# Neighbour attention's keys in groups of half a tile, and four smaller changes of order in a two-block transformer kernel

## Time and profile before

| | |
|---|---|
| three runs | 1334.83, 1334.91, 1335.91 us |
| the profiled execution's own time | 1333.72 us |
| its span in the trace | 1332.2 us |
| granted clock of PE, mean | 0.993 |
| PE busy | 1291.9 us, 97% of the span |
| DVE busy | 741.3 us, 56% |
| ACT busy | 474.2 us, 36% |
| POOL busy | 607.7 us, 46% |
| DMA | 105.40 MB, 79 GB/s in the mean |
| chain that ended last | PE 88%, DVE 4%, issue 3%, POOL 3%, ACT 1%, DMA 1% |

### The profile page before, as it was taken

One profiled execution on the slowest core, in us unless ns is written; L12 is line 12 of the kernel. 1 busy time (PEld: TensorE's weight loads), 2 busy tenths in 40 slices (PEclk: granted clock), 3 DMA queues, 4 the chain that ended last, 5 costly groups with the idle time before them and its releaser, 6 DMA issues.

```text
span 1332.2 us, 20250 instructions
## 1 busy us (share of the span) xinstructions
PE 1291.9 (97%) x6918; PEld 1050.4 (79%) x6918; DVE 741.3 (56%) x1372; ACT 474.2 (36%) x1010; POOL 607.7 (46%) x367
## 2 busy tenths in 40 slices
PE   7999999999899999999999999999999999999997
PEld 6877777877688888888888788888877888888765
DVE  4236867566855454533436677876526555555541
ACT  3233333422422222221114566666104444554520
POOL 5523323238354444445551444444367656666421
PEclk9999999999999999999999999999999999999999
DMA  6422222233233333332233211111143222222202
GB/s 179 113 59 83 65 79 64 64 89 107 65 108 89 99 90 99 90 102 88 87 103 96 63 50 32 47 47 48 35 134 106 62 76 76 75 64 74 63 26 69
DMA packets 196561, 105.40 MB, mean 79 GB/s; under 512 B 18982, under 2 KB 194444, under 8 KB 196508
## 3 DMA queue, kind: packets, MB, share of 16 engines
q1 hardware_dynamic: 196060, 104.00, 27.4%
q0 software_dynamic: 432, 0.69, 0.3%
q10 hardware_dynamic: 16, 0.00, 0.0%
HBM read 102.57 MB, written 2.10 MB: 79 GB/s over the span
## 4 chain that ended last, share of the span: by engine, by line
PE 88%; DVE 4%; issue 3%; POOL 3%; ACT 1%; DMA 1%; SPq 0%; DVEq 0%; POOLq 0%; ACTq 0%
PE ps L365 20%; PE ps L366 20%; PE ps L367 20%; PE ps L396 8%; POOL w_low L344 1%; PE ps L1389 1%; PE ps L1359 1%; PE ps L1370 1%; PE ps L1122 1%; PE ps L1392 1%; PE ps L1140 1%; PE ps L936 1%; PE ps L378 1%; PE ps L1141 1%; PE ps L1142 1%
## 5 line engine op out<-in xcount | busy, mean ns | idle before, releaser
L344 POOL TENSOR_TENSOR w_low<-w_raw,w_high 128x1024 fp32r<-128x1024 f32 x180 | 437.5, 2432 | 472.9 <-DVE w_high L339 461.0
L365 PE MATMUL ps<-h_high,w_high 128*128 128x512 f32 x816 | 333.1, 408 | 5.2 <-POOL w_low L344 3.7
L366 PE MATMUL ps<-h_low,w_high 128*128 128x512 f32 x816 | 323.6, 397 | 0.0
L367 PE MATMUL ps<-h_high,w_low 128*128 128x512 f32 x816 | 322.2, 395 | 0.0
L339 DVE CAST w_high<-w_raw 128x1024 fp32r<-128x1024 f32 x183 | 160.3, 878 | 98.1 <-DMA w_raw<-in_w_in_dram 36.7
L365 PEld LDWEIGHTS ps<-h_high,w_high 128*128 128x128 f32 x816 | 154.0, 189 | 46.5 <-issue 5.4
L367 PEld LDWEIGHTS ps<-h_high,w_low 128*128 128x128 f32 x816 | 154.2, 189 | 35.2
L366 PEld LDWEIGHTS ps<-h_low,w_high 128*128 128x128 f32 x816 | 154.1, 189 | 34.1 <-issue 2.6
L1654 ACT ACTIVATE z<-ps,cv 128x512 f32<-128x512 f32 x42 | 32.7, 778 | 156.3 <-PE ps L367 156.3
L2248 DVE SCALAR_TENSOR_TENSOR z<-ps,cv,z 128x511 f32<-128x511 f32 x42 | 31.5, 749 | 96.8 <-ACT z L1654 96.8
L366 PE MATMUL ps<-m_low,w_high 128*128 128x512 f32 x176 | 69.4, 395 | 0.0
(11 more groups left out here) (363 smaller groups left out, 2438.2 us busy)
## 6 DMA issues: line engine op xcount, KB each, us to landing
w_raw<-in_w_in_dram SPq DMA_DIRECT2D x150, 256.0 KB, 3.2
w_raw<-in_w_up_dram SPq DMA_DIRECT2D x88, 256.0 KB, 3.2
w_raw<-in_w_out_dram SPq DMA_DIRECT2D x44, 256.0 KB, 3.0
w_raw<-in_w_down_dram SPq DMA_DIRECT2D x32, 256.0 KB, 3.0
w_raw<-in_w_down_dram SPq DMA_DIRECT2D x16, 192.0 KB, 2.6
rel<-in_rel_bias_dram SPq DMA_DIRECT2D x8, 384.0 KB, 3.2
x_tok<-in_x_dram SPq DMA_DIRECT2D x4, 512.0 KB, 5.9
w_raw<-in_w_ob_dram SPq DMA_DIRECT2D x8, 256.0 KB, 2.9
```

The costliest lines, as they stand in the source:

```text
L344: pool.tensor_tensor(w_low[:, n % RING, :], w_raw[:, n % RAW, :], w_high[:, n % RING, :].bitcast(F32), ALU.subtract).then_inc(low_made, 1)
L365: pe.matmul(acc, wh, mh, start=first and k == 0, stop=False)
L366: pe.matmul(acc, wh, ml, start=False, stop=False)
L367: done = pe.matmul(acc, wl, mh, start=False, stop=last and k == tiles - 1)
```

## The change

- **Neighbour attention.** In a tile the tokens lie as (column, row), so that 8 columns are 64 tokens that follow one another. Each tile sees keys by half tiles: the widths with meta keys are 224, 272, 272 and 208. Keys are laid out once with the meta keys repeated between them (`nk_n`, 5 pieces); whole groups of 128 are 1, 2, 2, 1; what is left at either end, up to 80 rows with the meta keys, is turned as one group and weighed against `nv_end`. v is turned in three whole groups and two ends. The bias table has 6 additions for each head (4 of 128 elements, 2 of 64) that read and write with steps of 16 and 8 elements. In `weigh`, each half has two products over whole groups, of 256 and 128 columns, in place of three. `copy_b` waits for `turn`, no more for `copy_a`. Where the tokens are placed, loaded or stored (`x_t`, mask, `rel`, cos and sin, `out`) the order is changed to match; `rel` comes in a DMA for each head, and a store's outermost index is the column, 16 long.
- **Feed-forward.** DVE casts strip `N_UP+3` before `norm_dve`; in the first `up_turn` the casts are those of `N_UP+4`, `+5` and `+6`.
- **Last latent head.** `y_rounded` runs on each half; the low part is subtracted on DVE by halves (`m_y_rest`), no more on POOL.
- **POOL's order.** The wait for `tables_in` comes after the lows of `N_OM+6` and `N_OM+7`. In the first pair alone the table of the next pair stands behind `squares_low(i, c + 1, 0)`, not before it.

The diff, without buffer declarations, semaphore counts and blank lines:

```
-NA_W = [2 * P, 3 * P, 3 * P, 2 * P]
-NA_G = [0, 0, 1, 2]
-NA_OFF = [2 * META + 3 * P, 0, META, 3 * META + 5 * P]
-NA_COLS = 4 * META + 7 * P
-NA_WIN = [META, META, 0, 0]
-NA_META = [0, 0, 3 * P, 2 * P]
+HALF_TILE = P // 2
+END = META + HALF_TILE
+NA_W = [END + META + P, META + 2 * P, META + 2 * P, P + END]
+NA_K = [0, END, END + META + P, END + META + 2 * P]
+NA_KEYS = 2 * END + META + 3 * P
+NA_OFF = [0, END + META + P, END + 2 * META + P, END + 3 * META + 3 * P]
+NA_COLS = 2 * END + 3 * META + 4 * P
+NA_FULL = [1, 2, 2, 1]
+NA_WIN = [END + META, META, 0, 0]
+NA_META = [0, 0, 2 * P, P]
...
-return ps[:, 2:4, :].rearrange("p b (a h q) -> p (b a) h q", h=2, q=P)[:, 0:n]
+return ps[:, 2, 0:n * 2 * P].rearrange("p (a h q) -> p a h q", h=2, q=P)
...
+def half_tiles(ap, first, n):
+    dims = [[1, 8], [16, 8]]
+    if n > 1:
+        dims = [[P - 8, 2]] + dims
+    return bass.AP(tensor=ap.tensor, offset=ap.offset + first, ap=[list(d) for d in ap.ap[:-1]] + dims)
...
+def by_columns(ap):
+    return ap.rearrange("p (g r c) -> p g c r", r=8, c=16)
+def tiles(ap):
+    return ap.rearrange("p (g c r) -> p g c r", c=16, r=8)
...
-sp.dma_start(mask[:], c_mask).then_inc(s["tables_in"], 16)
+sp.dma_start(mask[:], c_mask.rearrange("(r c) k -> c r k", c=16)).then_inc(s["tables_in"], 16)
...
-sp.dma_start(rel[:], rel_bias[0:2].rearrange("h q k -> q h k")).then_inc(s["rel_in"], 16)
+for h in range(2):
+    sp.dma_start(rel[:, h, :], rel_bias[h].rearrange("(r c) k -> c r k", c=16)).then_inc(s["rel_in"], 16)
...
-dst = out[0].rearrange("(r g c) d -> g r c d", g=CG, c=16)[t]
+dst = out[0].rearrange("(r g c) d -> g c r d", g=CG, c=16)[t]
 sp.dma_start(dst[:, :, d], y_tok[:, t, d]).then_inc(s["out_stored"], 16)
...
-y_parts(3, 1)
...
 z_ = c % 2
...
-    for o, m, r in ((META, 0, 0), (NA_OFF[0] + META, 3 * P, P), (NA_OFF[3], 5 * P, 0)):
-        w = 3 * P if m == 0 else 2 * P
-        pool.tensor_tensor(nb[:, z_, h, o:o + w], rel[:, h, r:r + w],
-                           mask[:, m:m + w], ALU.add).then_inc(s["nb_ready"], 1)
-for o in (0, META + 3 * P, NA_OFF[0], NA_OFF[3] + 2 * P):
+    for o, m, r, n in ((NA_OFF[1] + META, 8, 8, 2), (NA_OFF[1] + META + P, P + 8, P + 8, 2),
+                       (END + META, 3 * P + 8, P + 8, 2),
+                       (NA_OFF[3], 5 * P + 8, 8, 2), (META, 3 * P, P, 1),
+                       (NA_OFF[3] + P + META, 5 * P + P + 8, P + 8, 1)):
+        to = nb[:, z_, h, o:o + n * HALF_TILE]
+        if n > 1:
+            to = to.rearrange("p (b c r) -> p b c r", c=8, r=8)
+        else:
+            to = to.rearrange("p (c r) -> p c r", r=8)
+        pool.tensor_tensor(to, half_tiles(rel[:, h, :], r, n), half_tiles(mask[:], m, n), ALU.add)\
+            .then_inc(s["nb_ready"], 1)
+for o in (0, NA_OFF[1], NA_OFF[2] + 2 * P, NA_OFF[3] + P):
     pool.tensor_copy(nb[:, z_, :, o:o + META],
...
 if more:
     ahead = N_NA + 4 * (c + 2)
-    bias_table(i, c + 1)
+    if c:
+        bias_table(i, c + 1)
     squares_low(i, c + 1, 0)
+    if c == 0:
+        bias_table(i, c + 1)
     make_low(pool, ahead, i * 8)
...
-pool.wait_ge(s["tables_in"], 64)
 for n in range(N_OM + 6, N_OM + 8):
     make_low(pool, n)
+pool.wait_ge(s["tables_in"], 64)
+pool.memset(np_end[:], 0.0)
+pool.memset(nb[:, :, :, END:END + META], -1e30)
 bias_table(0, 0)
...
-w, k0 = META + NA_W[t], (0, 0, META + P, META + 2 * P)[t]
...
 def turn(i, c, t):
     pe.wait_ge(s["t_probs"], i * 8 + (4 * c + t + 1))
     if c or t:
+        pe.wait_ge(s["t_copied_a"], i * 8 + (4 * c + t))
+    for a in range(NA_FULL[t]):
+        for h in range(2):
+            o = (2 * a + h) * P
+            k = NA_WIN[t] + a * P
+            pe.transpose(ps[:, 2, o:o + P], ne[:, t % 2, h, k:k + P], ident[:])
+    if c or t:
         pe.wait_ge(s["t_copied_b"], i * 8 + (4 * c + t))
-    for a in range(NA_W[t] // P):
-        for h in range(2):
-            o = (2 * a + h) % 4 * P
-            k = NA_WIN[t] + a * P
-            pe.transpose(ps[:, 2 + a // 2, o:o + P], ne[:, t % 2, h, k:k + P], ident[:])
     for h in range(2):
-        mm = pe.transpose(ps[0:META, 3, (2 + h) * P:(3 + h) * P],
-                          ne[:, t % 2, h, NA_META[t]:NA_META[t] + META], ident[:])
+        mm = pe.transpose(ps[0:NA_ENDS[t], 3, h * P:(1 + h) * P],
+                          ne[:, t % 2, h, NA_META[t]:NA_META[t] + NA_ENDS[t]], ident[:])
     mm.then_inc(s["t_turned"], 1)
...
-for a, q in ((0, slice(0, 2 * P)), (1, slice(0, 2 * P)), (2, slice(P, 2 * P))) if p == 0 else \
-        ((1, slice(0, 2 * P)), (2, slice(0, 2 * P)), (0, slice(0, P))):
+for a, q in (((0, slice(0, 2 * P)), (1, slice(P, 2 * P))), ((1, slice(0, 2 * P)), (0, slice(0, P))))[p]:
...
 def turn_v(i, c):
     pe.wait_ge(s["nv_kept"], i * 2 + (c + 1))
-    for a in range(4):
-        pe.transpose(ps[:, 5, a * P:(a + 1) * P], nvf[:, META + a * P:META + (a + 1) * P], ident[:])
-    pe.transpose(ps[0:META, 6, 0:P], nvf[:, 0:META], ident[:]).then_inc(s["nv_turned"], 1)
+    for a in range(3):
+        pe.transpose(ps[:, 5, a * P:(a + 1) * P], nvf[:, END + a * P:END + (a + 1) * P], ident[:])
+    for e, of in enumerate((nvf[:, 0:END], nvf_end[:])):
+        mm = pe.transpose(ps[0:END, 6, e * P:(e + 1) * P], of, ident[:])
...
-act.activation(x_t[:, k, :].rearrange("p (g r c) -> p r g c", g=CG, c=16),
+act.activation(x_t[:, k, :].rearrange("p (g c r) -> p r g c", g=CG, c=16),
...
+def y_rounded(i, c, q=slice(0, S)):
+    act.wait_ge(s["s_y"], i * 4 + (2 * c + q.stop // (2 * P)))
...
+y_rounded(i, c, slice(0, 2 * P))
 m_copy(i, c, 3)
...
-y_rounded(3, 1)
+y_rounded(3, 1, slice(2 * P, S))
...
-act.activation(halves(nvf), wide(5), ACT.Copy).then_inc(s["nv_kept"], 1)
+act.activation(halves(nvf), wide(5), ACT.Copy)
+act.activation(nvf_end[:, 0:META], ps[:, 5, 0:META], ACT.Copy)
+act.activation(nvf_end[:, META:END], ps[:, 6, HALF - HALF_TILE:HALF], ACT.Copy).then_inc(s["nv_kept"], 1)
...
+make_high(dve, N_UP + 3)
 norm_dve(dve, 2, xs, V_FFN, S, hh, hl)
...
-make_high(dve, N_UP + 4 * c + m + 3, i * 4)
+if c:
+    make_high(dve, N_UP + 4 * c + m + 3, i * 4)
+elif m < 3:
+    make_high(dve, N_UP + m + 4)
...
 dve.wait_ge(s["qr_turned"], i + (c // 2 + 1))
-dve.tensor_tensor(turned, ps[:, 7, :], sin[:, META:L], ALU.mult).then_inc(s["qr_part"], 1)
...
+def m_y_rest(q, n):
+    dve.wait_ge(s["s_high"], n)
+    dve.tensor_tensor(y_low[:, 7, q], gy[:, q], y_high[:, 7, q].bitcast(F32), ALU.subtract)\
...
+m_y_rest(slice(0, 2 * P), 8)
 m_gated(i, c, 1)
+m_y_rest(slice(2 * P, S), 9)
...
-dve.tensor_tensor(kpe_root, k_pe, cos[:], ALU.mult).then_inc(s["pe_part"], 1)
+dve.tensor_tensor(kpe_root[:, 0:META], k_pe[:, 0:META], cos[:, 0:META], ALU.mult)
+dve.tensor_tensor(tiles(kpe_root[:, META:L]), tiles(k_pe[:, META:L]), by_columns(cos[:, META:L]), ALU.mult).then_inc(s["pe_part"], 1)
...
-dve.tensor_tensor(halves(kpe_sq), wide(0), halves(sin[:]), ALU.mult).then_inc(s["pe_part"], 1)
+dve.tensor_tensor(kpe_sq[:, 0:META], ps[:, 0, 0:META], sin[:, 0:META], ALU.mult)
+for b, at, o in ((0, META, META), (1, META + 2 * P, 0)):
+    p = dve.tensor_tensor(tiles(kpe_sq[:, at:at + 2 * P]), tiles(ps[:, b, o:o + 2 * P]),
+                          by_columns(sin[:, at:at + 2 * P]), ALU.mult)
+p.then_inc(s["pe_part"], 1)
...
-dve.tensor_copy(np_meta[:, :, q], ps[0:META, 3, 2 * P:4 * P].rearrange("p (h q) -> p h q", h=2))\
+dve.wait_ge(s["t_turned"], i * 8 + (4 * c + t + 1))
+n = NA_ENDS[t]
...
 def normed(i, c, m):
     dve.wait_ge(s["q_root"], i * 8 + (4 * c + 2 * m + 2))
-    dst = (nk_f[:, 0:L], nq_f)[m]
-    dve.scalar_tensor_tensor(dst, dst, (col(V_NK), nq_gain[:, 0:1])[m], root[:, m, 0:(L, S)[m]],
-                             ALU.mult, ALU.mult).then_inc(s["q_normed"], 1)
-    if m == 0:
-        dve.wait_ge(s["q_normed"], i * 6 + (3 * c + 1))
-        dve.tensor_copy(nk_f[:, L:L + META], nk_f[:, 0:META]).then_inc(s["q_normed"], 1)
+    if m == 1:
+        dve.scalar_tensor_tensor(nq_f, nq_f, nq_gain[:, 0:1], root[:, 1, 0:S], ALU.mult, ALU.mult)\
+            .then_inc(s["q_normed"], 1)
+        return
+    for to, at, n in ((0, 0, END), (END + META, END, 3 * P), (NA_KEYS - HALF_TILE, L - HALF_TILE, HALF_TILE),
+                      (END, 0, META), (NA_KEYS - END, 0, META)):
+        nk = dve.scalar_tensor_tensor(nk_n[:, to:to + n], nk_f[:, at:at + n], col(V_NK),
+                                      root[:, 0, at:at + n], ALU.mult, ALU.mult)
+    nk.then_inc(s["q_normed"], 2)
```

More of the change, by code:

```diff
@@ L1089, in kpe_turn @@
                 pe.wait_ge(s["pe_part"], 2)
-                for h in range(2):
-                    mm = pe.matmul(ps[:, h, 0:HALF], rot[:], k_pe[:, h * HALF:(h + 1) * HALF], start=True, stop=True)
-                mm.then_inc(s["pe_turned"], 1)
+                cut = META + 2 * P
+                pe.matmul(ps[:, 0, 0:cut], rot[:], k_pe[:, 0:cut], start=True, stop=True)
+                pe.matmul(ps[:, 1, 0:L - cut], rot[:], k_pe[:, cut:L], start=True, stop=True).then_inc(s["pe_turned"], 1)
```

(2 more changed lines are left out.)

66 lines of the change are left out of this document (36 added, 30 removed).

## The result

The changed kernel took 1304.67 us in the median of four runs (1303.55 to 1305.26), the kernel before 1334.95 in the median of four, one more than above (1334.83 to 1335.91). The ratio is 0.9771 with a 95% interval of 0.9754 to 0.9788. Predicted were 1304.0, from 1299 to 1314. The span of the profiled execution went from 1332.2 to 1301.8 us, 30.4 less; the working had 30.7. That is closer than the terms behind it deserve: three of them were off by 1.0, 3.3 and 3.4 us, two effects that the sum did not have were worth +1.3 and −1.2, and all these cancel. The closeness of the total is luck.

A forecast was written before the change was run, and what follows sets the result against it. PE, busy 97% of 1332.2 us, was taken to set the end nearly everywhere. Terms summing to 30.7 us take the profiled execution from 1333.7 to 1303.0; with 1.2 added for the median, about 1304 us, range 1299 to 1314.

The forecast's parts named there:

- A: Neighbour attention pairs: fewer transposes, narrower scores and less weighing cut PE's work by 2.12 us a pair, 17.0 in eight.
- C: First pair: squares_low ahead of the table gives 3.45 us back, the second squares_low then comes 1.4 late: +2.1 us.
- D: Feed-forward: the earlier cast removes PE's 3.69 us wait for strip N_UP+3 and 1.71 of slow running behind it: 5.4 us.
- E: Latent tail and POOL's waits: last head's low part by halves +1.1 us, lows before the table wait +1.5: +2.6.
- F: Last pair: narrower tiles and copy_b no longer behind copy_a shorten the bare chain by 1.1 us (0.5 to 1.5).
- G: Output stores at the end: 16 columns outermost use all sixteen DMA engines, saving half of 6.8 us: +3.4.
- H: Added work elsewhere: key's rotary multiplication in five pieces with strided tables −0.7 us, later heads' rotary products −0.2.
- B: Loop of pairs: no other engine is late; POOL's bias table takes 6.2 us, PE waits only from 7.4: cost 0.
- rival 4: DVE's strided reads double and small waits stay in the last pair: 2.2 us more, 1306.4 us; 13%.
- The stores' rival: The output stores stay on half the DMA engines, so their gain falls away: 1307.6 us; 12%.
- The third: Rival: the bias table costs 7.5 to 9 us, so PE waits in seven pairs: 1310 to 1324 us; 10%.
- The first: Rival: POOL's bias table bounds the pair; additions over 11 us eat the gain, at 12 a pair 1343 us; 4%.

The follow-up runs named there:

- experiment 8: Changed kernel with bias, mask and rotary tables stored in order, 10 contiguous additions for 12, second table made before the first pair: 1297.08 us, ratio 0.9715.
- experiment 12: Changed kernel with each whole group of a tile turned twice, 96 more transposes in all: 1313.41 us, ratio 0.9843.
- experiment 3: Changed kernel with mask and relative bias already in the new order in memory, so the table's additions read contiguous elements: 1302.28 us, ratio 0.9762.
- experiment 10: Changed kernel with the last latent head rounded whole by ACT and its low part subtracted whole on POOL, as before: 1305.8 us, ratio 0.9789.
- experiment 6: Changed kernel with the cast of N_UP+3 back behind the normalisation and POOL's wait for tables_in back before the two lows: 1313.02 us, ratio 0.9843.
- experiment 4: Changed kernel with the second bias table made by heads in POOL's idle stretches before the first pair: 1300.89 us, ratio 0.9759.
- experiment 7: Changed kernel with the output stores walking 8 rows outermost, not 16 columns, so tokens land in wrong places: 1307.45 us, ratio 0.9801.

## Why the prediction was right, and which of its terms were not

| Term | predicted | measured, from the places and experiments |
|---|---|---|
| A, PE's work in eight pairs | +17.0 | +20.4 |
| C, first pair beside A | +2.1 | −1.2 |
| D, feed-forward | +5.4 | +5.6 |
| E, latent tail and POOL's wait | +2.6 | +2.6 |
| F, last pair beside A | +1.1 | +1.1 |
| low clock in the last product | none | +1.3 |
| G, stores | +3.4 | +3.6 |
| H, key's part and heads | −0.9 | −1.9 |
| start, in code not changed | none | −1.2 |
| sum | 30.7 | 30.3 of 30.4 |

A is eight times what a pair lost, C is 3.45 less the 4.6 of experiment 8, and F is what the places leave once A and C are taken off; the other rows are stretches between places.

**A was too small.** A pair lost 2.55 us, not 2.12. The timeline of PE in the changed kernel, with `weigh`, the turn of tile 2 (two whole groups) and of tile 3 (one):

```profile
1094.78 0.87 PE L1425 MATMUL ps<-np_,nv 128*64 128x256 f32 x8
...
1096.59 0.60 PE L1405 MATMUL ps<-ident,ne 128*128 128x128 f32 x4
...
1097.34 0.36 PE L1394 MATMUL ps<-nk_high,nq_high 64*128 64x208 f32 x2
...
1104.20 0.38 PE L1405 MATMUL ps<-ident,ne 128*128 128x128 f32 x2
1104.42 0.38 PE L1409 MATMUL ps<-ident,ne 128*80 128x128 f32 x2
1104.73 0.37 PE L1394 MATMUL ps<-nk_high,nq_high 64*128 64x224 f32 x2
...
1105.25 0.50 PE L387 MATMUL ps<-h_high,w_high 128*128 128x512 f32 x1
```

A turn with two whole transposes takes 1104.73 − 1104.20 = 0.53 us, one with four 1097.34 − 1096.59 = 0.75, where the earlier trace rows has 0.81 for four and 0.97 for six. I read the price of two transposes from the one difference that the kernel before offered, 0.16. It is 0.22 (experiment 12: 2 × 0.109), and four beside two ends are shorter now: turns gave 0.9 a pair in place of 0.64. The matmuls of `weigh` begin at 1094.78 and are through at 1096.01, 1.23 us with their ends, where it was 1.23 + 0.58: 1.16 a pair, not 0.96. Scores gave 0.45, not 0.52.

**B held for the table, not for all of POOL.** PE waits for no table in the loop at 6.4 to 6.5 us a table, between the 6.2 taken and the 7.4 from which it would. POOL in the loop before, and in the changed kernel:

```profile
1087.76 4.76 POOL L730 TENSOR_TENSOR nb<-rel,mask 128x384 f32<-128x384 f32 x6
```

```profile
1111.47 6.49 POOL L760 TENSOR_TENSOR nb<-rel,mask 128x128 f32<-128x128 f32 x12
...
1118.50 1.34 POOL L770 TENSOR_TENSOR y_low<-sq,y_high 128x528 fp32r<-128x528 f32 x1
```

The prediction named a rest of idle before `squares_low` as a sign. It did not come: the idle of 2.09 us is gone, as its own 6.2 against the 5.7 that cost nothing says. `squares_low` ends at 1119.84 and PE asks for it at 1120.67, so that 0.8 us of slack are left.

It also called a wait for `ne` in a pair a sign of being wrong, and that one did come at times. In four of the twelve profiles of the changed kernel and its variants one or two pairs of the loop, not always the same, have a wait of 0.5 to 0.7 us for `ne`. The row of it on DVE, from the repeat of the changed kernel:

```profile
1147.17 3.89 DVE L2599 TENSOR_SCALAR ne<-ne,nm 128x272 f32<-128x272 f32 x2
```

The two divisions of 0.3 us each take 3.89 while POOL adds, copies and subtracts without a break; they end at 1151.06, and POOL's last subtraction before a pause at 1150.91. The Trainium skill's "SBUF — State Buffer" (Who interferes with whom) says that DVE instructions of some kinds, `tensor_scalar` among them, can contend with POOL for a shared port pair, which one instruction holds to its end while the other is blocked. The 3.89 us agree with that; why the same divisions take 0.63 us in the first pair, at 1025.20, beside POOL's copies and a strip's low part, no run here shows.

**C is the step that failed most.** It had the right sequence, and the right place of the new wait, with the wrong sizes. The timeline of POOL, which answers to the earlier trace rows:

```profile
1016.55 1.32 POOL L770 TENSOR_TENSOR y_low<-sq,y_high 128x528 fp32r<-128x528 f32 x1 [1.89 <-ACT y_high L1955]
1017.84 7.21 POOL L760 TENSOR_TENSOR nb<-rel,mask 128x128 f32<-128x128 f32 x12
1025.00 0.90 POOL L763 COPY nb<-meta_b 128x32 f32<-128x32 f32 x4
1025.86 2.34 POOL L366 TENSOR_TENSOR w_low<-w_raw,w_high 128x1024 fp32r<-128x1024 f32 x1
1028.16 1.71 POOL L770 TENSOR_TENSOR y_low<-sq,y_high 128x512 fp32r<-128x512 f32 x1
```

Additions of 7.21 us in place of 6.2, copies 0.90 (0.6), and `squares_low` 1.71 (1.3): 1.7 us more, less 0.1 in the strip's low part, which makes 2.99 us of wait out of 1.4. The clock dip behind it (1.53 us), which I had only in the bad end of the bound, came too. −4.6 in place of −1.4.

Of the 1.0 us in the additions only 0.2 is the rate, since a table in the loop takes 6.4. The other 0.8 belongs to the first pair, and it stood in the rows of before: there too the table took 5.52 us, against 4.76 in the loop. The prediction set 5.52 beside its 6.2 and did not carry the difference over. In that pair the 128-element additions take 746 ns in the mean, against 644 in the table from 1111.47 on. What makes them longer there was not tested.

The step itself costs what experiment 3 shows, a factor of 1.6 against the contiguous 2.2 ns. The prediction's middle of the two rates was in effect a factor of 1.5. The Trainium skill's "GPSIMD Engine Reference" (Performance pitfalls for Q7 kernels) has half as much again, and by it an estimated 6.3 us a table; the loop's 6.4 to 6.5 agree within 0.2, the first pair's 7.21 do not, and for one element the 1.6 measured here decides. At the unchanged rate the prediction gives back 0 in one sentence and 0.3 in another; its own sum gives 0.2.

**D, E, F, G** came out within 0.2 us each, F as a remainder whose parts no run measures. E's first part is 1.0 (experiment 10). Its second is 1.6 against the kernel before, with its shorter table, though it is worth 3.3 once the long one is there (experiment 6).

**H was too small.** It went halfway to rival 4: DVE's multiplications cost half as much again, not double. At the first head the longer chain (1.41 us of wait) cost nothing, as a wait of 0.39 just behind it went away. In the other heads it cost 0.61 for every two, which I had called 0.2 in all. The multiplication by sin is 0.36 us longer and stands on DVE ahead of the next tile's maximum, for which ACT's exponential waits, and behind that ACT's squares and DVE's copy to `q_f`, for which PE then waits 0.21. That is 0.37 with the start behind it; the other 0.25 shows in no row as a wait.

**The clock.** The prediction said that each wait of PE of over 1.5 us inside the kernel costs more than itself. In the fourteen profiles that is so behind all but one of the waits of 1.8 us and more, but not behind those of 1.64 and 1.70 us (experiments 4 and 6). And it overlooked that the wait of 1.43 us in the last product had a low clock behind it as well, the +1.3 of the table.

**What the rivals were worth.** The stores' rival fell by experiment 7. The third (a table of 7.5 us or more) nearly happened in the first pair, not in the loop. The first is far off: to eat the 31 us gained, seven pairs would have to lose 4.4 each, 2.7 of wait and 1.7 of clock. By the 7.4 from which PE waits that is a table of 10.1 us, some 4 longer than measured. The prediction wrote 5.6 and 11 there; the sum was off, the conclusion was not.
